# GLA decoder layer: two tiles of key decays and two of query decays, used in turn

## The reference, cut to what matters

```python
b = jnp.cumsum(gb, axis=2)                       # log decays, cumulated in the chunk
rel = jnp.exp(jnp.where(causal, b[:, :, :, None, :] - b[:, :, None, :, :], -jnp.inf))
attn = jnp.einsum('bhtd,bhsd,bhtsd->bhts', qb, kb, rel)
o = (jnp.einsum('bhtd,bhdv->bhtv', qb * jnp.exp(b), S)
     + jnp.einsum('bhts,bhsv->bhtv', attn, vb))
S = (jnp.exp(b_last)[..., None] * S
     + jnp.einsum('bhsd,bhsv->bhdv', kb * jnp.exp(b_last[:, :, None, :] - b), vb))
```

## Time and profile before

| | |
|---|---|
| median of 3 runs | 2595.76 us |
| profiled execution | 2597.05 us |
| its span in the profile | 2595.3 us |
| granted TensorE clock, mean | 0.996 |
| busy: PE, PEld | 98%, 82% |
| busy: DVE, ACT, POOL | 60%, 46%, 17% |
| POOL busy | 449.6 us, 411 instructions |

### The profile page before, as it was taken

How to read it: one execution, slowest core, us unless ns; L and a number is a source line. 1 busy time by engine, 2 the same in 40 slices (tenths; PEclk the granted TensorE clock), 3 DMA queues, 4 the chain that set the end, 5 groups by cost and what they waited for, 6 DMA issues and landing times.

```text
span 2595.3 us, 34642 instructions
## 1 busy us (share of the span) xinstructions
PE 2536.1 (98%) x11968; PEld 2121.1 (82%) x11968; DVE 1545.8 (60%) x2255; ACT 1205.5 (46%) x1752; POOL 449.6 (17%) x411
## 2 busy tenths in 40 slices
PE   6999999999999999999999999999999999999998
PEld 6788887888788888888878888888887888888886
DVE  5466457556646745666556664556665565465666
ACT  4534344544544435455444443545455444354444
POOL 4134444000004420000000541000000254000000
PEclk8999999999999999999999999999999999999999
DMA  7522367544422123543442213254443222334443
GB/s 277 167 82 66 147 210 265 189 130 149 170 88 66 65 99 97 178 147 131 131 162 82 65 66 114 89 188 147 148 143 124 73 65 68 112 131 161 147 159 133
DMA packets 191879, 339.41 MB, mean 131 GB/s; under 512 B 7024, under 2 KB 118768, under 8 KB 183504
## 3 DMA queue, kind: packets, MB, share of 16 engines
q1 hardware_dynamic: 188768, 328.36, 38.0%
q10 hardware_dynamic: 2928, 8.66, 0.8%
HBM read 311.84 MB, written 25.17 MB: 130 GB/s over the span
## 4 chain that ended last, share of the span: by engine, by line
issue 49%; PE 40%; DVE 4%; POOL 3%; ACT 2%; DMA 1%; DVEq 0%; POOLq 0%; ACTq 0%; SPq 0%
PE banks L1567 11%; PE banks L1569 10%; PE banks L1568 10%; PE banks L1713 3%; PE banks L1693 1%; POOL queries L696 1%; POOL h_lo L721 1%; PE banks L1752 1%; PE banks L1754 1%; PE banks L1737 1%; DVE w_lo L1109 1%; POOL rstd L654 1%; DMA raw<-in_w_kv 1%; DVE sr L1307 0%; DVE u_lo L1475 0%
## 5 line engine op out<-in xcount | busy, mean ns | idle before, releaser
L1567 PE MATMUL banks<-h_hi,w_hi 128*128 128x512 f32 (+1 forms) x1760 | 678.4, 385 | 16.7 <-DVE h_lo L1128 4.9
L1569 PE MATMUL banks<-h_hi,w_lo 128*128 128x512 f32 (+1 forms) x1760 | 669.3, 380 | 0.0
L1568 PE MATMUL banks<-h_lo,w_hi 128*128 128x512 f32 (+1 forms) x1760 | 669.3, 380 | 0.0
L1109 DVE TENSOR_TENSOR w_lo<-raw,w_hi 128x2048 fp32r<-128x2048 f32 x144 | 349.7, 2429 | 299.6 <-ACT w_hi L757 299.6
L757 ACT ACTIVATE w_hi<-raw 128x2048 fp32r<-128x2048 f32 x144 | 275.5, 1913 | 272.6 <-PE banks L1567 233.8
L1567 PEld LDWEIGHTS banks<-h_hi,w_hi 128*128 128x128 f32 x1760 | 332.2, 189 | 84.1 <-issue 23.1
L1569 PEld LDWEIGHTS banks<-h_hi,w_lo 128*128 128x128 f32 x1760 | 331.9, 189 | 63.2
L1568 PEld LDWEIGHTS banks<-h_lo,w_hi 128*128 128x128 f32 x1760 | 332.2, 189 | 61.0
L1567 PE MATMUL banks<-w_hi,u_hi 128*128 128x512 f32 x896 | 351.8, 393 | 0.7 <-DVE w_lo L1116 0.7
L1569 PE MATMUL banks<-w_hi,u_lo 128*128 128x512 f32 x896 | 349.1, 390 | 0.0
L1568 PE MATMUL banks<-w_lo,u_hi 128*128 128x512 f32 x896 | 348.8, 389 | 0.0
(11 more groups left out here) (166 smaller groups left out, 3153.5 us busy)
## 6 DMA issues: line engine op xcount, KB each, us to landing
raw<-in_w_up SPq DMA_DIRECT2D x64, 1024.0 KB, 5.4
raw<-w_mix SPq DMA_DIRECT2D x64, 1024.0 KB, 4.7
raw<-in_gla_w_in SPq DMA_DIRECT2D x57, 1024.0 KB, 5.0
raw<-in_w_down SPq DMA_DIRECT2D x48, 1024.0 KB, 4.6
raw<-in_w_out SPq DMA_DIRECT2D x24, 1024.0 KB, 4.9
xin<-in_x SPq DMA_DIRECT2D x5, 2048.0 KB, 10.9
xin<-in_w_down SPq DMA_DIRECT2D x10, 1024.0 KB, 4.9
w_mix<-xin SPq DMA_DIRECT2D x10, 1024.0 KB, 9.8
```

The costliest lines, as they stand in the source:

```text
L1109: nc.vector.tensor_tensor(w_lo[:, i % 2, :], raw[:, i % 2, :], w_hi[:, i % 2, :].bitcast(F32), ALU.subtract).then_inc(lo_split.sem, PIECES)
L1567: after_chunk(pe.matmul(to, left[0], right[0], start=start, stop=False, skip_group_check=goes_on))
L1568: pe.matmul(to, left[0], right[1], start=False, stop=False, skip_group_check=goes_on)
L1569: return pe.matmul(to, left[1], right[0], start=False, stop=stop, skip_group_check=goes_on)
```

## The change

`key_dec` and `query_dec` become lists of two tiles each. The second ones lie behind `v`, in the range of `u_parts`. Decay `e` uses tile `e % 2`, in the gaps, the exponentials and the products. The gaps of decay `e` now wait for product `e - 2` instead of `e - 1`, and so does the exponential of the end query decay; `end_gap` (`e` is the key decay) waited for the product two ahead already and still does. Since the second tiles lie in slot 2 of the tiles that are stored in the first block, VectorE and ScalarE each get one more wait on those stores, behind the gaps and decays of the first rung and ahead of the loop over half-steps.

```diff
-            key_dec = mx("key_dec", [P, HEADS, P])
-            query_dec = mx("query_dec", [P, HEADS, COLS])
+            key_dec = [mx("key_dec", [P, HEADS, P])]
+            query_dec = [mx("query_dec", [P, HEADS, COLS])]
...
+            key_dec.append(mx("key_dec_2", [P, HEADS, P]))
+            query_dec.append(mx("query_dec_2", [P, HEADS, COLS]))
@@ GpSimd, rung_products @@
+                at = (c * DECAYS + rung - 1) % 2
                 pool.wait_ge(*decay_ready.at(n, c * DECAYS + rung - 1))
                 w = SPANS[rung - 1]
-                nc.gpsimd.tensor_tensor(keys[:], at_chunk(k_, c), key_dec[:], ALU.mult)
+                nc.gpsimd.tensor_tensor(keys[:], at_chunk(k_, c), key_dec[at][:], ALU.mult)
@@ GpSimd, end_products @@
-                for e, tensor, decays in ((QUERY_DECAY, q, query_dec[:, :, 0:P]), (KEY_DECAY, k_, key_dec[:])):
+                for e, tensor, decays in ((QUERY_DECAY, q, query_dec[(c * DECAYS + QUERY_DECAY) % 2][:, :, 0:P]),
+                                          (KEY_DECAY, k_, key_dec[(c * DECAYS + KEY_DECAY) % 2][:])):
@@ ScalarE, end_decays @@
-                    act.wait_ge(*product_ready.at(n, c * DECAYS + QUERY_DECAY - 1))
+                    e = c * DECAYS + QUERY_DECAY
+                    act.wait_ge(*product_ready.at(n, e - 2))
@@ ScalarE, ahead of its half-steps @@
                 near_decays(0)
                 rung_decays(0, 1)
+                act.wait_ge(mix_stored[2], 16 * sum(mix_slot(j) == 2 for j in range(MIX_STEPS)))
@@ VectorE, rung_gaps @@
-                    if e:
-                        dve.wait_ge(*product_ready.at(n, e - 1))
+                    if e > 1:
+                        dve.wait_ge(*product_ready.at(n, e - 2))
                     each = "p h (m w) -> p h m w"
                     nc.vector.tensor_tensor(
-                        key_dec[:].rearrange(each, w=w),
+                        key_dec[e % 2][:].rearrange(each, w=w),
@@ VectorE, end_gap @@
-                    dve.wait_ge(*product_ready.at(n, c * DECAYS + QUERY_DECAY - 1))
-                    nc.vector.tensor_tensor(key_dec[:], b[:, :, P - 1:P].broadcast_to([P, HEADS, P]), b,
+                    e = c * DECAYS + KEY_DECAY
+                    dve.wait_ge(*product_ready.at(n, e - 2))
+                    nc.vector.tensor_tensor(key_dec[e % 2][:], b[:, :, P - 1:P].broadcast_to([P, HEADS, P]), b,
@@ VectorE, ahead of its half-steps @@
                 rung_gaps(0, 1)
+                dve.wait_ge(mix_stored[2], 16 * sum(mix_slot(j) == 2 for j in range(MIX_STEPS)))
```

More of the change, by code:

```diff
@@ L375, in build @@
         w2_raw = b_[0:3 * PAIR, 0, :]
-        masks_raw = query_dec[:].rearrange("p h t -> p (h t)")[:, 0:(RUNGS - 1) * COLS + ODD]
+        masks_raw = query_dec[0][:].rearrange("p h t -> p (h t)")[:, 0:(RUNGS - 1) * COLS + ODD]
         scan_raw = scratch[:, 1, :]
@@ L691, in rung_products @@
                     return
+                at = (c * DECAYS + rung - 1) % 2
                 pool.wait_ge(*decay_ready.at(n, c * DECAYS + rung - 1))
                 w = SPANS[rung - 1]
-                nc.gpsimd.tensor_tensor(keys[:], at_chunk(k_, c), key_dec[:], ALU.mult)
+                nc.gpsimd.tensor_tensor(keys[:], at_chunk(k_, c), key_dec[at][:], ALU.mult)
                 for kind, (first, count, _) in enumerate(KINDS):
                     last = nc.gpsimd.tensor_tensor(kind_cols(queries, w, kind), spans(at_chunk(q, c), w, first, count),
-                                                   kind_cols(query_dec, w, kind), ALU.mult)
+                                                   kind_cols(query_dec[at], w, kind), ALU.mult)
                 last.then_inc(product_ready.sem, 1)
@@ L854, in rung_decays @@
                     act.wait_ge(*gap_ready.at(n, c * (DECAYS - 1) + rung - 1))
-                    nc.scalar.activation(key_dec[:], key_dec[:], ACT.Exp, scale=1.0 / TAU)
-                    nc.scalar.activation(query_dec[:], query_dec[:], ACT.Exp, scale=1.0 / TAU)\
+                    at = (c * DECAYS + rung - 1) % 2
+                    nc.scalar.activation(key_dec[at][:], key_dec[at][:], ACT.Exp, scale=1.0 / TAU)
+                    nc.scalar.activation(query_dec[at][:], query_dec[at][:], ACT.Exp, scale=1.0 / TAU)\
                         .then_inc(decay_ready.sem, 1)
                 def end_decays(c):
-                    act.wait_ge(*product_ready.at(n, c * DECAYS + QUERY_DECAY - 1))
-                    nc.scalar.activation(query_dec[:, :, 0:P], at_chunk(b_, c), ACT.Exp, scale=1.0 / TAU)\
+                    e = c * DECAYS + QUERY_DECAY
+                    act.wait_ge(*product_ready.at(n, e - 2))
+                    nc.scalar.activation(query_dec[e % 2][:, :, 0:P], at_chunk(b_, c), ACT.Exp, scale=1.0 / TAU)\
                         .then_inc(decay_ready.sem, 1)
                     act.wait_ge(*gap_ready.at(n, c * (DECAYS - 1) + QUERY_DECAY))
-                    nc.scalar.activation(key_dec[:], key_dec[:], ACT.Exp, scale=1.0 / TAU).then_inc(decay_ready.sem, 1)
+                    at = (c * DECAYS + KEY_DECAY) % 2
+                    nc.scalar.activation(key_dec[at][:], key_dec[at][:], ACT.Exp, scale=1.0 / TAU)\
+                        .then_inc(decay_ready.sem, 1)
                     nc.scalar.activation(chunk_decay[:, c, :], b_[:, :, (c + 1) * P - 1], ACT.Exp, scale=1.0 / TAU)\
@@ L1238, in rung_gaps @@
                     for kind, (first, count, _) in enumerate(KINDS):
-                        last = nc.vector.tensor_tensor(kind_cols(query_dec, w, kind), spans(b, w, first, count),
+                        last = nc.vector.tensor_tensor(kind_cols(query_dec[e % 2], w, kind), spans(b, w, first, count),
                                                        span_end(b, w, first - 1, count), ALU.subtract)
```

## The result

| | before | after |
|---|---|---|
| median | 2595.89 us (22 runs) | 2599.49 us (22 runs) |
| ratio of the times | 1 | 1.0015 (95%: 1.0009 to 1.0022) |
| profiled execution, its span | 2597.05, 2595.3 us | 2601.91, 2600.1 us |
| TensorE's wait at the rung scores | 7.1 us in 8 waits | 10.4 us in 12 waits |
| busy: VectorE, GpSimd | 1545.8, 449.6 us | 1578.8, 466.4 us |

The change makes the kernel 3.6 us slower. Ratios compare executions at a granted TensorE clock of 0.995 to 0.997; two of run 9's ten, at 0.75 and 0.65, are left out of its ratio.

A forecast was written before the change was run, and what follows sets the result against it. TensorE, busy 98%, bounds it; only about 9 us of pauses could go. Half-steps 5 and 6 cost 0.95 us, half-step 9 0.8: 1.75 per block, times 4 = 7.0, median 2602.8 us; likeliest 2600 to 2606, 80% range 2592.5 to 2612.

The forecast's parts named there:

- the opened ring: Rung stage: VectorE's gaps wait for GpSimd's previous product, products for ScalarE's exponentials, exponentials for gaps; the change opens this.
- rival 3: The engines take turns everywhere: half-step 5 costs 1.4 us, the sum is 1.3 per block, 5.2 in all, 2601; chance 25%.
- The bound: TensorE's late rung scores at half-steps 5, 6 and 9: about 2.2 us per block, 9 in all, at most to gain.
- (a): Rung stage: gaps stop waiting for the product ahead; only one wait per engine is added, no duration changes by itself.
- (b): Gaps now run beside GpSimd's rung products and lengthen them by the gaps' whole length; range nothing to 2.0 us per product.
- Rival 1: Gap instructions cost GpSimd nothing: half-step 6's scores come 1.05 us earlier per block, 4.2 in all, 2591.6; chance 12%.
- (c): Half-step 5: gaps begin ahead of the product and VectorE holds on for 2.0 us, so the scores come 1.8 us later.
- (d): Half-step 6: its product starts earlier but still has the weight split inside; the step gives back 0.85 of 1.8 us.
- Half-step 9: In turns, a key gap (0.55 us) and one query gap (0.3) come into the product; scores 0.8 us later.
- Elsewhere: Half-step 2 has room for one key gap (0.7 into 1.3 us); half-steps 10 to 15 for 1.7 us more.
- (e): New wait on the store of slot 2, counting only in the first block: free, by 4 us.
- the signs named for "wrong": VectorE or ScalarE standing at the store wait; products beside gaps keeping 1.3 and 2.1 us; TensorE's rung-score wait below 7.

The follow-up runs named there:

- run 9: The changed kernel with the three query gaps ahead of the key gap in every rung; ratio to the kernel before 1.0009.
- runs 5 and 6: VectorE's rung gaps ahead of the weight split in all even half-steps, on the kernel before (one tile) and the changed one (two): ratios 0.9963 and 0.9957.
- run 2: The changed kernel with rung and near gaps as reductions with one SBUF input instead of two, for timing only; ratio to the kernel before 0.9983.
- run 1: The changed kernel with second tiles and store wait kept, but gaps and end query decay waiting for product e - 1 again; ratio to the kernel before 1.0003.
- runs 4 to 6: Rung gaps ahead of the weight split: kernel before, half-steps 4, 8, 12 (ratio 0.9967); all even half-steps, kernel before (0.9963) and changed kernel (0.9957).

## Why the prediction was right, and one term too large

The direction and its reason were right: gaps that run beside products lengthen them, and this costs more than the opened ring gives. The size was not: 3.6 us against 7.0, inside the 80% range but just below the 2600 to 2606 that the likeliest case gave itself. At half-step 5 the trace shows the turns of rival 3 (5.2 us, given 25%) and not the holding that the forecast had assumed.

**The bound.** TensorE's three late rung scores per block were all that moved; everything behind them shifted by the same amount. Right, with a ceiling read a little too low: 9 us were read from the earlier trace rows, and the stages of runs 5 and 6 are 10.1 us shorter than before. Half-step 6 had been compared with an interval of 6.87, which was itself 0.12 longer than the 6.75 that they reach.

**(a), (b): gaps beside products cost the products time.** Right, and shown by run 2 together with the row of L1280 beside it. Rival 1, by which they cost nothing, gave -4.2 us; run 2, which makes it true, is at -4.4 (0.9983) and -5.5 in the stages. So the rival's arithmetic was about right and its condition false.

**(c) half-step 5.** Forecast 1.8 us later, measured 0.96 (8.12 - 7.16). This is the mis-sized term. It charged the whole 2.0 us of the gaps, on the ground of the earlier trace rows, where VectorE holds the port through a run. At half-step 5 they take turns: the key product is held for 0.45 us and the query products for 0.5, and the near gap finds the last of them under way and waits itself. Turns at every instruction, as in rival 3, had been put at 1.4, nearer but still too much. The reason is that a gap fitted between two products doesn't cost them its full length. The three query instructions of half-step 5, shortest, middle and longest in ns, on GpSimd before and after and on VectorE before and after:

```profile
L696 POOL TENSOR_TENSOR queries<-q,query_dec x3: 464/735/1013, 822.7 to 824.3; 128x384 f32<-128x384 f32 x1, 128x256 f32<-128x256 f32 x1, 128x128 f32<-128x128 f32 x1
...
L699 POOL TENSOR_TENSOR queries<-q,query_dec x3: 498/904/1330, 825.1 to 827.2; 128x384 f32<-128x384 f32 x1, 128x256 f32<-128x256 f32 x1, 128x128 f32<-128x128 f32 x1
...
L1239 DVE TENSOR_TENSOR query_dec<-b x3: 286/418/552, 825.4 to 826.2; 128x384 f32<-128x384 f32 x1, 128x256 f32<-128x256 f32 x1, 128x128 f32<-128x128 f32 x1
...
L1248 DVE TENSOR_TENSOR query_dec<-b x3: 805/1234/1641, 823.9 to 826.6; 128x384 f32<-128x384 f32 x1, 128x256 f32<-128x256 f32 x1, 128x128 f32<-128x128 f32 x1
```

The product instructions grow by 0.32, 0.17 and 0.03 us, behind gaps that alone take 0.55, 0.42 and 0.29, and the key product by 0.45 beside one of 0.69: each time about 0.24 less than the gap. The split is alike: it costs the product of half-step 6 about 2.0 of its 2.29 us.

**(d) half-step 6.** Forecast 0.85 given back, measured 0.81 (8.53 - 7.72), with the split and one key gap in the product as worked out: the product was put at 5.9 us and is 5.9. Half-step 9: forecast 0.8, measured 0.75. Elsewhere no loss: right.

**(e) the wait on the store.** Free: in the first block the store was issued at 135.14, VectorE was done with the first gaps at 147.9, some 4 us behind the store's landing, and its next instruction came when ScalarE's split was done, after 3.31 idle us as before; run 1 has the wait and not the loss.

**Sum.** Per block 0.96 - 0.81 + 0.75 = 0.90, times 4 = 3.6 us, against 1.75 and 7.0. With (c) at its measured size, and the rest as forecast, 0.95 + 0.8 - 0.85 = 0.9 per block gives 2595.8 + 3.6 = 2599.4, which is what was measured. At 3.6 us the kernel is slower, but by less than the 0.2% (5.2 us) that the forecast held likelier than not; 22 runs on each side tell it from zero.

**Its own signs.** Of those named for "right", the waits on L696 are gone, TensorE has more than 8 waits at the rung scores, the largest at half-step 5, and the interval from 5 to 6 is 7.7. The sizes that hung on (c) missed: the product of half-step 5 is 4.35 us and not 5.4, its key part 1.74 and not over 3, TensorE waits 10.4 us in all and not 14, and 1.2 at half-step 5 and not 2.2. None of the signs named for "wrong" came.

**What the prediction did not see** is that the order of VectorE's queue, not the ring, was at fault (runs 4 to 6). It had written down that half-step 5 hung on the split in front of the gaps, and that the split stood in the product of half-step 6, and it still took the order of the queue as given.

## What to carry to other kernels

A wait between two engines can be the very thing that keeps them out of each other's way. Before taking it away, ask what the freed instructions will run beside, and read the price where such a pair already meets, from one instruction's duration alone and beside the other. And when a product is late, look first at what stands ahead of its input in the other engine's queue: moving a long instruction behind short ones gained 0.37% here, where the second buffer lost 0.15%.

## What the runs showed of the hardware

- VectorE subtracting two SBUF tensors and GpSimd multiplying from SBUF hold each other up, and VectorE loses more by it: three query gaps took 3.53 us instead of 1.09, the products beside them 4.35 instead of 3.4. In the whole execution VectorE's busy time rose by 33 us and GpSimd's by 17, with no instruction more. A reduction with one SBUF input and the same output costs GpSimd nothing and is hardly held up (0.72 us, elsewhere mostly 0.67). A `tensor_tensor` with one of its two inputs in PSUM costs GpSimd nothing either (the kernel before, shown at run 2).
- In such turns a VectorE instruction between two of GpSimd's costs GpSimd its own length less about 0.24 us, from gaps of 0.29 us to the split of 2.29.
- Who goes next at the end of a VectorE instruction isn't one rule: beside the near product (held for 0.94 us) VectorE went on through two or more instructions, at half-step 5 the two changed places at each. What decides it stays open; the order of the gaps does not (run 9). That the near product's 1.69 us is a held port, and not a slow start after 84 us of idleness, run 2 shows: with one-input gaps it takes 0.75 us after the same idle time.
